# Prompt attention of a hybrid decoder step: scores kept in their bank, a third pair of banks, and the engines' work turned around

## The reference

```
z = einsum('bqhd,bkhd->bhqk', q, k) * HEAD_DIM ** -0.5 + bias
mask = kpos < qpos
log_1m = where(mask, log_sigmoid(-z), 0.0)
between = cumsum(log_1m, axis=3, reverse=True) - log_1m
weights = exp(where(mask, log_sigmoid(z) + between, -inf))
out = einsum('bhqk,bkhd->bqhd', weights, v)
```

## Time and profile before

| | us |
|---|---|
| median of three runs | 2207.02 |
| lowest and highest | 2203.86, 2209.66 |
| the profiled execution | 2215.02 |
| its span | 2213.4 |
| PE busy in the span | 1986.6 (90%) |
| DVE, ACT, POOL busy | 865.7, 603.6, 350.2 |
| prompt attention, first scores to last outputs | 392.2 to 525.7 |

### The profile page before, as it was taken

The page is one execution under the profiler, slowest core; times in us unless marked ns, Lnnn a source line. Parts: engine busy times, 40 slices in busy tenths (PEclk is TensorE's granted clock), DMA queues, the critical chain, the costliest instruction groups (busy, mean ns, idle before and its releaser), DMA issues.

```text
span 2213.4 us, 34027 instructions
## 1 busy us (share of the span) xinstructions
PE 1986.6 (90%) x13955; PEld 1651.1 (75%) x13955; DVE 865.7 (39%) x1340; ACT 603.6 (27%) x1402; POOL 350.2 (16%) x562
## 2 busy tenths in 40 slices
PE   5999999999998787648888599699999999999996
PEld 4999899445997665247875244498888999888895
DVE  7111110442305764843334234533444333343435
ACT  3111111553223554322221012222222222222223
POOL 6300111333124465210000000100000000000004
PEclk9999999998556755678785599899999999999998
DMA  5111221202331111000000121111111211111112
GB/s 151 45 41 40 68 72 44 60 1 76 96 96 40 28 28 28 0 12 1 2 2 1 65 98 34 48 39 38 46 49 38 57 38 38 38 51 43 39 37 81
DMA packets 103828, 100.06 MB, mean 45 GB/s; under 512 B 15522, under 2 KB 89906, under 8 KB 103714
## 3 DMA queue, kind: packets, MB, share of 16 engines
q1 hardware_dynamic: 91266, 81.15, 12.5%
q0 software_dynamic: 6720, 17.11, 2.6%
q10 hardware_dynamic: 5728, 0.19, 0.2%
HBM read 85.78 MB, written 12.65 MB: 44 GB/s over the span
## 4 chain that ended last, share of the span: by engine, by line
PE 82%; DVE 9%; issue 3%; ACT 2%; POOL 2%; DMA 1%; POOLq 0%; ACTq 0%; SPq 0%; DVEq 0%
PE ps L416 17%; PE ps L417 17%; PE ps L418 17%; PE ps L2355 5%; PE ps L1226 2%; PE ps L814 2%; PE ps L851 2%; PE ps L613 1%; PE ps L619 1%; PE ps L1921 1%; PE ps L1895 1%; DVE arena L1144 1%; DVE arena L2016 1%; PE ps L1301 1%; DVE arena L2514 1%
## 5 line engine op out<-in xcount | busy, mean ns | idle before, releaser
L416 PE MATMUL ps<-h_split,w_split 128*128 128x384 f32 (+1 forms) x768 | 251.1, 327 | 3.4 <-DVE w_split L2498 3.4
L418 PE MATMUL ps<-h_split,w_split 128*128 128x384 f32 (+1 forms) x768 | 250.9, 327 | 0.0
L417 PE MATMUL ps<-h_split,w_split 128*128 128x384 f32 (+1 forms) x768 | 250.7, 326 | 0.0
L2525 DVE TENSOR_TENSOR arena<-arena,ps 128x1024 f32<-128x1024 f32 x144 | 175.5, 1219 | 164.4 <-PE ps L418 164.4
L417 PE MATMUL ps<-w_split,u_split 128*128 128x512 f32 (+1 forms) x576 | 224.5, 390 | 0.0
L416 PE MATMUL ps<-w_split,u_split 128*128 128x512 f32 (+1 forms) x576 | 224.4, 390 | 0.0
L418 PE MATMUL ps<-w_split,u_split 128*128 128x512 f32 (+1 forms) x576 | 224.3, 389 | 0.0
L2506 DVE TENSOR_TENSOR u_split<-above_u_split,u_split 128x384 fp32r<-128x384 f32 (+1 forms) x96 | 51.5, 536 | 295.8 <-ACT above_u_split L2479 295.7
L2458 ACT ACTIVATE w_split<-below_w_split 128x1024 fp32r<-128x1024 f32 x64 | 64.1, 1048 | 340.4 <-PE ps L418 321.7
L416 PEld LDWEIGHTS ps<-h_split,w_split 128*128 128x128 f32 x768 | 144.7, 188 | 5.1 <-issue 3.6
L416 PE MATMUL ps<-h_hi,w_split 128*128 128x384 f32 (+3 forms) x432 | 141.9, 329 | 6.0 <-DVE w_split L528 6.0
(11 more groups left out here) (377 smaller groups left out, 3758.1 us busy)
## 6 DMA issues: line engine op xcount, KB each, us to landing
below_w_split<-in_w_up SPq DMA_DIRECT2D x32, 512.0 KB, 4.7
below_w_split<-in_w_down SPq DMA_DIRECT2D x32, 512.0 KB, 4.0
w_raw<-in_w_in SPq DMA_DIRECT2D x27, 512.0 KB, 3.9
arena<-in_x_prompt SPq DMA_DIRECT2D x16, 512.0 KB, 3.8
arena<-in_cache_sb_k SPq DMA_DIRECT2D x64, 128.0 KB, 2.1
arena<-in_cache_sb_v POOLq DMA_DIRECT2D x64, 128.0 KB, 2.3
nat_scratch<-nat_stage POOLq DMA_DIRECT2D x32, 128.0 KB, 2.0
arena<-nat_scratch SPq DMA_DIRECT2D x16, 256.0 KB, 3.6
```

The lines of the kernel that those rows point to most:

```text
L416: pe.matmul(out, w_hi, x_hi, start=first, stop=False)
L417: pe.matmul(out, w_hi, x_lo, start=False, stop=False)
L418: return pe.matmul(out, w_lo, x_hi, start=False, stop=last)
L2525: dve.tensor_tensor(y_acc[0:r, i, :], y_acc[0:r, i, :], p, ALU.add).then_inc(S("dn_out"), 1)
```

## The change

The score matmul leaves its accumulation open (`stop=False`), and the terms of the exponent are added on top of the scores in the same bank. The second making of the scores (L605) is gone. Since a bank then holds a block from its scores until its weights are made, the pairs of banks 0 to 5 are used in turn, `2 * (n % 3) + c`: three blocks instead of two pairs for scores and one pair for exponents. S(n) now waits for W(n-3). E(n) changes the bank of scores, so it may start only when SP(n) has read it: the wait for `sb_sp` stands at its start, ahead of all its matmuls, and so do the waits for the sum and the mask. Inside E(n) the matmuls go head by head instead of term by term. PE's loop is E(n), S(n+2), O(n-1). DVE's stream is C(0), C(1), then SP(n), C(n+2). ACT's is exp and log of 0 and 1, then W(n), exp and log of n+2. POOL's function is the same.

```diff
--- before.py
+++ after.py
@@ -587,35 +587,28 @@
 
             def scores(n):
                 pr, G, kt, q0, w, c0, hg = sb_geometry(n)
-                if n >= 2:
-                    pe.wait_ge(S("sb_sp"), n - 1)
+                if n >= 3:
+                    pe.wait_ge(S("sb_w"), n - 2)
                 for c in range(2):
                     rws = slice(64 * c, 64 * c + 64)
-                    ins = pe.matmul(ps[:, 2 * (n % 2) + c, 0:w], skT[rws, pr, kt * P:kt * P + P],
-                                    sqT[rws, pr, q0:q0 + w], start=True, stop=True)
+                    ins = pe.matmul(ps[:, 2 * (n % 3) + c, 0:w], skT[rws, pr, kt * P:kt * P + P],
+                                    sqT[rws, pr, q0:q0 + w], start=True, stop=False, skip_group_check=True)
                 ins.then_inc(S("sb_z"), 1)
 
             def exponents(n):
                 pr, G, kt, q0, w, c0, hg = sb_geometry(n)
-                banks = [ps[:, 4 + c, 0:w] for c in range(2)]
-                if n >= 1:
-                    pe.wait_ge(S("sb_w"), n)
-                for c, bank in enumerate(banks):
-                    rws = slice(64 * c, 64 * c + 64)
-                    pe.matmul(bank, skT[rws, pr, kt * P:kt * P + P], sqT[rws, pr, q0:q0 + w], start=True,
-                              stop=False, skip_group_check=True)
-                if kt >= 4 * G:
-                    for bank in banks:
-                        pe.matmul(bank[:, 0:P], ident, neg_big, start=False, stop=False, skip_group_check=True)
+                pe.wait_ge(S("sb_sp"), n + 1)
                 if kt < 4 * G + 3:
                     pe.wait_ge(S("sb_sum"), n)
-                    for c, bank in enumerate(banks):
+                if kt >= 4 * G:
+                    pe.wait_ge(S("sb_spm"), sb_diagonals(n))
+                for c in range(2):
+                    bank = ps[:, 2 * (n % 3) + c, 0:w]
+                    if kt >= 4 * G:
+                        pe.matmul(bank[:, 0:P], ident, neg_big, start=False, stop=False, skip_group_check=True)
+                    if kt < 4 * G + 3:
                         pe.matmul(bank, neg_ones, sb_sum[:, (n - 1) % 2, c, c0:512], start=False, stop=False,
                                   skip_group_check=True)
-                pe.wait_ge(S("sb_sp"), n + 1)
-                if kt >= 4 * G:
-                    pe.wait_ge(S("sb_spm"), sb_diagonals(n))
-                for c, bank in enumerate(banks):
                     pe.matmul(bank, neg_tri, sb_sp[:, n % 3, c, 0:w], start=False, stop=True,
                               skip_group_check=True).then_inc(S("sb_x"), 1)
 
@@ -636,27 +629,31 @@
             scores(0)
             scores(1)
             for n in range(SBN):
+                exponents(n)
                 if n + 2 < SBN:
                     scores(n + 2)
-                exponents(n)
                 if n >= 1:
                     outputs(n - 1)
             outputs(SBN - 1)
 
         def sb_vector(dve):
             dve.wait_ge(S("params"), 16 * N_PAR_DMA)
-            for n in range(SBN):
+
+            def clipped(n):
                 pr, G, kt, q0, w, c0, hg = sb_geometry(n)
-
                 dve.wait_ge(S("sb_z"), n + 1)
                 for c in range(2):
                     h = 2 * pr + c
-                    ins = dve.tensor_scalar(sb_zc[:, n % 2, c, 0:w], ps[:, 2 * (n % 2) + c, 0:w],
+                    ins = dve.tensor_scalar(sb_zc[:, n % 2, c, 0:w], ps[:, 2 * (n % 3) + c, 0:w],
                                             sb_bias[:, h:h + 1], 40.0, ALU.add, ALU.min)
                 ins.then_inc(S("sb_zc"), 1)
-                if n >= 1:
-                    softplus(dve, n - 1)
-            softplus(dve, SBN - 1)
+
+            clipped(0)
+            clipped(1)
+            for n in range(SBN):
+                softplus(dve, n)
+                if n + 2 < SBN:
+                    clipped(n + 2)
 
         def softplus(dve, n):
 
@@ -667,7 +664,7 @@
                 dve.wait_ge(S("sb_sum"), n - 2)
             for c in range(2):
                 h = 2 * pr + c
-                ins = dve.scalar_tensor_tensor(sb_sp[:, n % 3, c, 0:w], ps[:, 2 * (n % 2) + c, 0:w],
+                ins = dve.scalar_tensor_tensor(sb_sp[:, n % 3, c, 0:w], ps[:, 2 * (n % 3) + c, 0:w],
                                                sb_bias[:, h:h + 1], sb_zc[:, n % 2, c, 0:w], ALU.add, ALU.max)
             ins.then_inc(S("sb_sp"), 1)
             if kt >= 4 * G:
@@ -685,7 +682,7 @@
                 for c in range(2):
                     h = 2 * pr + c
                     act.wait_ge(S("sb_x"), 2 * n + c + 1)
-                    ins = act.activation(sb_w[:, n % 2, c, 0:w], ps[:, 4 + c, 0:w], ACT.Exp,
+                    ins = act.activation(sb_w[:, n % 2, c, 0:w], ps[:, 2 * (n % 3) + c, 0:w], ACT.Exp,
                                          bias=sb_bias[:, h:h + 1])
                 ins.then_inc(S("sb_w"), 1)
                 if n >= 1 and SB_BLOCKS[n - 1][2] == 0:
@@ -696,17 +693,21 @@
                 act.wait_ge(S("sb_pv"), n + 1)
                 act.activation(mixT[:, 4 + pr, 512 * G:512 * G + 512], ps[:, 6 + hg % 2, :], ACT.Copy)\
                     .then_inc(S("sb_o"), 1)
-            for n in range(SBN):
+
+            def log_sums(n):
                 w = sb_geometry(n)[4]
                 zc = sb_zc[:, n % 2, :, 0:w]
                 act.wait_ge(S("sb_zc"), n + 1)
                 act.activation(zc, zc, ACT.Exp).then_inc(*did("act"))
                 act.wait_ge(*so_far("act"))
                 act.activation(zc, zc, ACT.Ln, bias=one_col).then_inc(S("sb_l"), 1)
-                if n >= 2:
-                    weights(n - 2)
-            weights(SBN - 2)
-            weights(SBN - 1)
+
+            log_sums(0)
+            log_sums(1)
+            for n in range(SBN):
+                weights(n)
+                if n + 2 < SBN:
+                    log_sums(n + 2)
             finished(SBN - 1)
 
         def sb_gpsimd(pool):
```

## The result

The changed kernel takes 2238.67 us (median of four runs, 2233.89 to 2258.96), the kernel before 2207.24 (median of four). The two medians stand 31.4 us apart, a quotient of 1.0142; the ratio estimated from all the runs is 1.0172, interval 1.0134 to 1.0210. The forecast was 2234, slower. Its profiled execution took 2233.89 us with a span of 2232.3, so the two traces stand 18.9 us apart; the other runs of it are longer.

What follows compares the result with a forecast made beforehand. PE bounds the stage before; the change makes a closed line through DVE. Line +23.7 and clock +3 give +26.7, added to the 2207.0 median: about 2234 us, slower; range 2218 to 2264, the forecast's own 2222 to 2248.

Steps and rivals of the forecast that it cites:

- the closed line: Prompt attention after the change: E(n), S(n+2), C(n+2), SP(n+1), mask where diagonal, E(n+1); only O(n-1) covers DVE, 1.01 against 2.78 us.
- the signs named: If right: turns of about 7.5 us, some 20 exponent waits of 1.9 us, outputs off chain, stage 157 to 160 us.
- The turn of a wide block: Wide block: exponents 3.64, scores 1.06, clip and softplus 2.73, plus hand-offs: 7.52 us for 6.57, +0.95.
- The load that I thought might fall into the wait: Unhidden weight load, 0.2 us by which L613 exceeds L619, might fall into PE's wait: 0 to -3 us, taken as 0.
- The line over the stage: From E(0) to the end of E(23): 152.0 us, so E(23) ends at 547.5 for 523.85, +23.7 us.
- What was costed at nothing: In the stage: weights before S(n+3), ACT's exp and log behind weights, POOL's sum, head-by-head order; all taken as covered or free.
- allow for 6 us of PE work in the narrow blocks that take twice as long: Clock term: 6 us of PE work in the stage's narrow blocks at 1.2 GHz, priced at half, +3 us.
- The rival's stretch at 720 to 740: Profile stretch of small matmuls, PE busy 15.12 of 20 us, granted clock 0.66 on average; would cost 47 us.
- that rival: Clock falls again and again in the stage: 15 to 47 us on top of 23.7, middle +55, 2262 us; chance 0.17.
- as it was: All stages behind prompt attention come 24 us later and are otherwise unchanged.
- PE the bound: Rival: clip and softplus find cover in wide blocks, L605's 15.5 us come off, 2191.5 us; chance 0.04.
- the shorter line: Rival: DVE takes a third less while PE stands, 19 us off, +4.7 to +8, 2212 to 2215 us; chance 0.05.

Runs made afterwards that it cites:

- TensorE's old order: Changed kernel with scores n+2 put back ahead of exponents n on TensorE: 2193.93 us (median of 10 runs), ratio 0.9954; last softplus matmul ends at 508.60.
- the pair of late and early wait: Kernel before, TensorE and ScalarE orders turned, scores made twice: softplus wait late, 2205.55 us (stage end 526.59); wait early, 2266.66 us (592.66).
- waits filled: Changed kernel with extra unused matmuls behind the outputs of all but the last three blocks: 2232.14 us, ratio 1.0101; last softplus matmul ends at 549.83.
- 11 in the second: Second trace: changed kernel run again with no edit, 2242.4 us (4 runs), ratio 1.0155; last softplus matmul ends at 563.45.
- the early wait alone: Kernel before with exponents waiting for softplus and mask at their start: last softplus matmul ends at 524.69, +0.8.
- TensorE's order alone: Kernel before with scores n+2 behind exponents n on TensorE: 2320.63 us, stage end +116; with ScalarE's order also turned, 2205.55 us, +2.7.

## Why the prediction was right, and where not

- The bound and the closed line. Right. PE is alone on the chain before; E, S, clip, softplus, E stand on it after. This is shown by the chain, by 1.0101 with the clock nearly held, by 0.9954 with TensorE's old order, and by the pair of late and early wait. Of the signs named, the turn and the waits came as said (23 waits of 2.0 us on average, for some 20 of 1.9); the stage lasted 171 us (391.8 to 562.6), not 157 to 160.
- The turn of a wide block: 7.52 forecast, 7.60 measured. The exponents took 1.13 for the first pair also when they started from a wait. The load that I thought might fall into the wait didn't: in the timeline PEld's L610 starts at 462.57, with the matmul, after a wait of 2.70 us for the same softplus.
- The line over the stage: +23.7 forecast. With waits filled it is 549.83 - 523.85 = 26.0, in which the filling itself has a part: in four blocks, where scores of 128 or 256 queries have just been made, it lasts longer than the wait did. From these scores to the next exponents it is 2.92, 3.12, 2.92 and 2.92 us, for 2.45, 2.68, 2.69 and 2.68 without it, 1.4 us in all; apart from one block that half clock made longer, the others agree within 0.02. So the line is about 24.6 us, less up to 1.7 for the 3.4 us still at half clock.
- What was costed at nothing: weights, exp and log, POOL's sum. Right for the change: PE's matmuls waited for softplus and mask in the changed stage, and the profile puts none of their waits down to the running sum or to ScalarE's log and weights. That ScalarE's turn was needed for this I had not seen; I had read the change to TensorE's order as the whole of it.
- The clock. The step "allow for 6 us of PE work in the narrow blocks that take twice as long", priced at +3, is the term that was mis-sized. It is not right in itself either: 6 us of work that take twice as long cost 6 us, not half of them. Measured, waits filled against not filled, it is +10.9 and +13.6, and with the filling's own 1.4 us about 12 and 15 (27 and 34 us at half clock, in wide blocks as well as narrow ones). I took the row at 398 to 400 us, one stretch of a single wait, for a stage in which a wait comes in every block. The rival's stretch at 720 to 740 was nearer in kind, though its size, 0.66, was not reached: 0.92 and 0.90. That is just short of the sign that I had named for that rival, under about 0.9, and the cost is at the foot of its 15 to 47 us. The rival's mechanism, a clock that falls again and again, is what happened; at the size of my own term it didn't.
- Everything behind the stage "as it was". Wrong in time, not in work: against the trace of the kernel before, the other stages gave back 18 us in the first trace and 11 in the second, at another granted clock. Much of this is the length of that one trace of the kernel before; between the stage's 36.8 and the medians' 31.4 it is 5.4. That still hid about half of the 10.1 us by which the stage lies above the 26.7 forecast. That the forecast of the whole was within 5 us of the median, nearer than the stage's terms were, is luck.
- PE the bound, and the shorter line: neither. The first is what the version with the old order shows, 2194 us, near the 2191.5 worked out for it. Against the second stand DVE's groups, as long after as before. The reading that I had set against it was weak: POOL's instruction ended at 443.08, so the clip ran beside it for only 0.37 of its 1.41 us.

That the clock of the later stages falls where it does by chance of timing is argued from the twelve traces (1671.6 to 1689.5 us behind the stage) and the scatter of runs (2196 to 2213 for the kernel before alone), not shown by an experiment. What decides it in one execution stays open.

## What to carry to other kernels

When work is taken off a bound engine and its order is turned in the same step, write down the closed line of waits for the new order and ask what still lies beside each piece. A third buffer helps only if something is issued early enough to fill it. An instruction's position in its queue and the place of a wait must be judged together, and on all engines of the loop: here the early wait alone cost 0.8 us, TensorE's order alone cost 2.7 us with ScalarE turned and 116 without. A matmul engine that began to wait a little in every turn lost clock here too. The loss showed in the stage and was partly hidden in the total, so compare stages before totals, and don't take one trace's later stages for the kernel's.

## What the runs showed of the hardware

- TensorE's granted clock fell to half again and again (27 us of 169 in one trace, 34 of 171 in the other) in a stage in which it was busy 73% of the time with float32 matmuls and its matmuls waited 2.8 us for DVE at the longest. Matmuls whose results nobody reads, put into the waits, brought that to 3.4 us and took 10.3 us off the whole.
- The same 32 small matmuls took 3.62 or 6.65 us by the granted clock. Over twelve traces the stages behind, which nothing touched, took 1671.6 to 1689.5 us.
